# A two-layer streaming encoder on one core: the differential layer's attention scored in head pairs, on a new slot plan, with one row-maximum instruction a pair and a new order of the output projection

## The chip, the cores and the metric

One core of a Trainium2 chip runs the whole program. The metric is the device time of one execution in microseconds, the median of several runs. The profiled execution is one more run, and the rows below come from it.

## What is computed

One inference step of two layers over 576 frames (512 of a prompt, 64 new frames of a running stream with 256 cached ones), width 1024. Layer 0 uses differential attention, layer 1 forgetting attention; each is followed by a SwiGLU FFN.

```python
# layer 0 (of each chunk-causal group of queries)
qkv = h @ w_qkv
q, k = _rope(...), _rope(...)
s = einsum('bqhd,bkhd->bhqk', q, k) * (DIFF_QK_DIM ** -0.5)      # 16 half heads of 64
p = softmax(where(allowed, s, -inf)).reshape(b, DIFF_HEADS, 2, tq, tk)
a = p[:, :, 0] - lam * p[:, :, 1]
o = einsum('bhqk,bkhe->bqhe', a, v)                               # 8 heads, 128 wide
o = rmsnorm(o, subln_w) * (1.0 - lam_init)
x = x + o.reshape(b, t, DIFF_V_WIDTH) @ w_o
x = x + (silu(gate) * up) @ w_out      # gate, up = split(rmsnorm(x) @ w_in)
```

## The kernel before

All matmul operands are split in a high part (fp32r) and a low rest, and a product is hi x hi + lo x hi + hi x lo. Activations lie as columns: 8 tiles of 128 features x 576 frames. Weights come in units of 8 blocks of 128 x 128 through two buffers. For each unit SP loads `w_raw`, ACT makes `w_hi` (`split`, called by `lead`, L787), POOL makes `w_lo` (`lead`, L1069), and PE uses it (`slice_`, L486): per block six matmuls of 288 columns. A slot is one such block. A buffer is free again when PE has used its unit, so hi and lo of unit n + 1 are made while PE is in unit n.

Both attention layers go over 8 groups g of 128 features: three units (k, q, v) in 24 slots, and into the slots of group g the attention of group g - 1 is put, by hand. `S_AT` gives the slots of the ten score jobs: five query blocks i in the order 4, 3, 2, 1, 0 with 384, 512, 384, 256 and 128 keys, for each of the two half heads. `T_AT` gives the slots of the transposes of p, and so on. The engines hold the same order each in its own program and meet by semaphores only. Each engine works strictly in the order of its program, so an instruction that waits holds up all that stand behind it.

One score job of layer 0 (`score`, L534 to L542): three matmuls with 64 rows (partitions 0 to 63 or 64 to 127) into bank jj % 2 of `sps`, then the mask with 128 rows. DVE takes the row maximum (`row_max`, L1233), ACT the exponential with its sum (`exps`, L866). After the second half head DVE weighs and subtracts the two (`weigh`: reciprocal of both, L1248, L1252). PE transposes the result (L554), ACT and DVE take the high part (`take_p`, L882) and the rest (`p_lo`, L1269). There are four buffers `pr`. The head's output is normed: `o_square` on POOL, `head_norm_sum` on PE (L604), `head_scale` on ACT, `norm_o` and `split_o` on DVE, `o_hi` on ACT. k and q of the next group pass `take_k`, `swap`, `rotate`, `k_hi`, `k_lo` and the same for q.

The output projection of a layer is 64 blocks, in the order of `WO_STEPS` (run, output tile, k), in 8 units. A run accumulates in one of two banks, and its end is added to x by DVE (`residual`, L1173); a run opens when the run before the last has been added. Blocks of head 7 (k = 7) come last. The norm for the FFN needs, tile by tile, `prep`: on ACT `xh` (L805), then, once `acc` holds the tile before, the square into the single buffer `sqt` (L809); on DVE `xl` (L1159) and `acc` += `sqt` (L1164). `norm_sum` (L505) adds `acc` over the partitions, `scale_of_norm` makes the factor `rs`. In ACT's program of before, the order at the end is prep of tile 0, lead(u + 6), preps 1 to 4, lead(u + 7), preps 5 to 7, lead(u + 8); lead(u + 7) is the first FFN unit.

## Time and profile before

| | us |
|---|---|
| median of 3 runs | 1607.16 (1603.75 to 1608.9) |
| the profiled execution | 1607.57 |
| its span, first to last instruction | 1605.4 |
| PE busy | 1563.1 (97%) |
| DVE, ACT, POOL busy | 619.9, 560.9, 581.5 |
| granted TensorE clock, mean | 0.991 |

The shares of the span say which engine is full on average. Where it isn't, the stretches and the timeline say what it waits for. In a timeline row "x2" joins two instructions that follow each other; two 288-column matmuls shown as 0.42 us overlap in the pipeline, and the distance from one row's start to the next is what they cost PE.

### The profile page before, as it was taken

How to read it: one execution, taken by the hardware profiler on the slowest of the kernel's cores; microseconds unless marked ns; L12 is line 12 of the kernel's file. 1: busy time of each engine (PE TensorE's matmuls, PEld its weight loads, DVE VectorE, ACT ScalarE, POOL GpSimd, SP SyncE). 2: the span in 40 equal slices, each digit the busy share in tenths (PEclk: the TensorE clock that was granted, in tenths of full speed). 3: DMA queues.
4: the chain of work that ended last, by engine and by line, in shares of the span. 5: the costliest groups of instructions: out<-in, count | busy, mean ns of one | idle time of the engine just before them, and what ended most of it. 6: DMA issues, size and time to landing. Idle time of an engine off the chain costs nothing.

```text
span 1605.4 us, 29879 instructions
## 1 busy us (share of the span) xinstructions
PE 1563.1 (97%) x11071; PEld 1476.8 (92%) x11071; DVE 619.9 (39%) x1091; ACT 560.9 (35%) x995; POOL 581.5 (36%) x276
## 2 busy tenths in 40 slices
PE   6999999999999999999999999999999999999996
PEld 5888888999999999999978888888999999999996
DVE  6667776451111111121366666665521111111212
ACT  4455545442222222222334444444332222232221
POOL 3333233334544444333322222221344455444331
PEclk9999999999999999999999999999999999999998
DMA  5322223122222222222211211111122222222222
GB/s 188 98 85 83 95 85 107 41 79 79 78 82 88 78 78 85 76 82 85 94 62 61 62 60 60 60 57 48 67 79 85 85 78 78 91 78 74 83 83 82
DMA packets 44628, 128.49 MB, mean 80 GB/s; under 512 B 5648, under 2 KB 10256, under 8 KB 44576
## 3 DMA queue, kind: packets, MB, share of 16 engines
q1 hardware_dynamic: 44576, 127.79, 23.6%
q8 instruction: 34, 0.56, 0.1%
q14 instruction: 18, 0.15, 0.0%
HBM read 111.21 MB, written 11.83 MB: 77 GB/s over the span
## 4 chain that ended last, share of the span: by engine, by line
PE 91%; DVE 5%; issue 2%; ACT 1%; DMA 1%; SPq 0%; DVEq 0%; ACTq 0%
PE ps L486 73%; PE sps L534 3%; PE ops L597 3%; PE tps L554 2%; PE sps L540 2%; PE sps L535 2%; PE sps L536 2%; PE sps L542 1%; PE ops L587 1%; DVE acc L1164 1%; DVE aug_l L1303 1%; DVE xT L1173 0%; PE tps L568 0%; DVE ptl L1269 0%; PE ops L604 0%
## 5 line engine op out<-in xcount | busy, mean ns | idle before, releaser
L1069 POOL TENSOR_TENSOR w_lo<-w_raw,w_hi 128x1024 fp32r<-128x1024 f32 (+1 forms) x199 | 469.4, 2359 | 922.2 <-ACT w_hi L787 922.2
L486 PE MATMUL ps<-xh,w_hi 128*128 128x288 f32 x2176 | 489.5, 307 | 18.5 <-DVE xl L1418 11.5
L486 PE MATMUL ps<-xl,w_hi 128*128 128x288 f32 x2176 | 468.7, 297 | 0.0
L486 PE MATMUL ps<-xh,w_lo 128*128 128x288 f32 x2176 | 468.3, 297 | 0.0
L486 PEld LDWEIGHTS ps<-xh,w_hi 128*128 128x128 f32 x2176 | 350.2, 191 | 20.4 <-issue 19.9
L787 ACT ACTIVATE w_hi<-w_raw 128x1024 fp32r<-128x1024 f32 (+1 forms) x200 | 208.3, 1042 | 451.7 <-PE ps L486 449.5
L486 PEld LDWEIGHTS ps<-xh,w_lo 128*128 128x128 f32 x2176 | 352.9, 190 | 0.0
L486 PEld LDWEIGHTS ps<-xl,w_hi 128*128 128x128 f32 x2176 | 352.8, 190 | 0.0
L866 ACT ACTIVATE pr<-sps,nmax 128x384 f32<-128x384 f32 (+3 forms) x160 | 85.9, 537 | 205.4 <-DVE nmax L1233 188.4
L486 PE MATMUL ps<-hh,w_hi 128*128 128x288 f32 x704 | 150.9, 295 | 0.0
L486 PE MATMUL ps<-hl,w_hi 128*128 128x288 f32 x704 | 150.8, 295 | 0.0
L486 PE MATMUL ps<-hh,w_lo 128*128 128x288 f32 x704 | 150.7, 295 | 0.0
L1179 DVE TENSOR_TENSOR uf<-ps,rs 128x576 f32<-128x576 f32 x44 | 33.4, 758 | 238.7 <-PE ps L486 238.7
L1487 DVE TENSOR_TENSOR hl<-hf,hh 128x576 f32 (+1 forms) x44 | 33.4, 758 | 228.7 <-ACT hh L1036 228.7
L1173 DVE TENSOR_TENSOR xT<-ps,xT 128x576 f32<-128x576 f32 (+1 forms) x40 | 30.2, 756 | 232.0 <-PE ps L486 231.7
L486 PEld LDWEIGHTS ps<-hl,w_hi 128*128 128x128 f32 x704 | 113.8, 188 | 0.0
L486 PEld LDWEIGHTS ps<-hh,w_hi 128*128 128x128 f32 x704 | 113.7, 188 | 0.0
L486 PEld LDWEIGHTS ps<-hh,w_lo 128*128 128x128 f32 x704 | 113.5, 188 | 0.0
L1233 DVE TENSOR_REDUCE nmax<-sps 128x1 f32<-128x384 f32 (+3 forms) x160 | 79.5, 500 | 88.0 <-PE sps L542 87.6
L1036 ACT ACTIVATE hh<-hf 128x576 f32 (+1 forms) x44 | 30.2, 686 | 178.3 <-POOL hf L1126 178.3
L534 PE MATMUL sps<-kh,qh 64*128 64x384 f32 (+3 forms) x160 | 66.8, 418 | 2.7 <-ACT qh L837 1.3
L1126 POOL TENSOR_TENSOR hf<-sg,uf 128x576 f32<-128x576 f32 x44 | 62.7, 1426 | 0.0
(154 smaller groups left out, 1768.6 us busy)
## 6 DMA issues: line engine op xcount, KB each, us to landing
w_raw<-w_units SPq DMA_DIRECT2D x184, 512.0 KB, 3.2
w_raw<-w_units SPq DMA_DIRECT2D x16, 384.0 KB, 2.8
qsw<-qsin SPq DMA_DIRECT2D x64, 72.0 KB, 2.0
xT<-x_in SPq DMA_DIRECT2D x8, 288.0 KB, 5.6
dk_out<-kf SPq DMA_DIRECT2D x8, 288.0 KB, 2.1
dv_out<-vf SPq DMA_DIRECT2D x8, 288.0 KB, 4.1
fk_out<-kf SPq DMA_DIRECT2D x8, 288.0 KB, 4.1
fv_out<-vf SPq DMA_DIRECT2D x8, 288.0 KB, 4.0
```

The costliest lines, as they stand in the source:

```text
L486: mm = nc.tensor.matmul(out[:, half, :], w[:, k, :], rhs[:, kt, half * HALF:(half + 1) * HALF], start=start and w is w_hi[slot] and rhs is ...
L534: nc.tensor.matmul(out, qh[par][b, q], kh[par][b, k], start=True, stop=False)
L535: nc.tensor.matmul(out, qh[par][b, q], kl[par][b, k], start=False, stop=False)
L536: nc.tensor.matmul(out, ql[par][b, q], kh[par][b, k], start=False, stop=False)
L597: mm = nc.tensor.matmul(ops[:, P * j:SEQ], v[:, j, :], p[:, j, P * j:SEQ], start=j == 0 and v is vh and p is pth, stop=j == 3 and v is vl)
L787: nc.scalar.activation(w_hi[slot][:, 0:kts, :], w_raw[slot][:, 0:kts, :], ACT.Copy).then_inc(w_hi_done, 1)
L866: nc.scalar.activation(pr[:, slot, 0:width(i)], sps[:, jj % 2, 0:width(i)], ACT.Exp, bias=nmax[:, slot:slot + 1], accum_out=den[:, slot:sl ...
L1069: nc.gpsimd.tensor_tensor(w_lo[slot][:, 0:kts, :], w_raw[slot][:, 0:kts, :], w_hi[slot][:, 0:kts, :].bitcast(F32), ALU.subtract).then_inc( ...
L1126: nc.gpsimd.tensor_tensor(hf[:], sg[:], uf[:], ALU.mult).then_inc(hf_done, 1)
L1179: tt(halves(dst), proj(n.c % 2), halves(scale), ALU.mult).then_inc(ps_read, 1)
L1233: nc.vector.tensor_reduce(nmax[:, slot:slot + 1], sps[:, jj % 2, 0:width(i)], AX_X, ALU.max, negate=True).then_inc(max_done, 1)
L1487: tt(at(hl, jt), hf[:], at(hh, jt).bitcast(F32), ALU.subtract).then_inc(hl_done, 1)
```

## The change

The first layer's attention gets its own program on every engine, written out for all 8 groups, on a time line t of slots; the second keeps its loops. In layer 0:

- `score_pair` scores both half heads in one slot, matmul by matmul in turn, then both masks. It starts when the exps of the pair before are done. Slots 2, 6, 10, 14, 18.
- `pair_max` takes both heads' row maxima with one reduction over both banks.
- the weighing takes the two reciprocals apart: `weigh_first` needs the first exp only.
- transposes of v stand at slot 6, of p at 8, 12, 16, 20, 24; the p x v product of the prompt at slot 27, the head's norm at 34 to 38, all counted from the start of the attention's own period; the small norm matmul goes to `tps[:, 3]`.
- `lead` on ACT and POOL stands at the second slot of each unit.

In both layers:

- `WO_STEPS` has 14 runs instead of 12, in another order. Counted from 0, runs 6 to 13 (tiles 0 to 7) end at steps 46, 47, 48, 49, 51, 53, 55 and 63.
- `prep` is spread among the steps (`wo_prep`, `wo_residuals`, `wo_finish`).
- `norm_sum` of the FFN stands in its second unit at k = 2 instead of its first at k = 6; that of layer 1 behind the first unit instead of at k = 6.

```diff
-WO_STEPS = ([(j, 2 + j, k) for j in (0, 1) for k in range(6)] + [(0, 2, 6), (1, 3, 6)]
-            + [(j, 2 + j, k) for j in (2, 3) for k in range(7)]
-            + [(4 + t, t, k) for t in (0, 1) for k in range(7)] + [(4 + t, t, 7) for t in range(6)]
-            + [(4 + t, t, k) for t in (6, 7) for k in range(KT)])
-WO_OPEN = [next(q for q, s in enumerate(WO_STEPS) if s[0] == j) for j in range(12)]
-WO_END = [max(q for q, s in enumerate(WO_STEPS) if s[0] == j) for j in range(12)]
-WO_EARLY = 9
+N_WO, N_IN, N_OUT, N_LAYER = 24, 38, 82, 90
+WO_STEPS = ([(j, 4 + j, k) for j in (0, 1, 2) for k in range(6)]
+            + [(j, j - 2, k) for j in (3, 4, 5) for k in range(7)]
+            + [(6, 0, k) for k in range(KT)]
+            + [(6 + t, t, 7) for t in (1, 2, 3)]
+            + [(6 + t, t, k) for t in (4, 5, 6) for k in (6, 7)]
+            + [(13, 7, k) for k in range(KT)])
+WO_RUNS = 14
+WO_OPEN = [next(q for q, s in enumerate(WO_STEPS) if s[0] == j) for j in range(WO_RUNS)]
+WO_END = [max(q for q, s in enumerate(WO_STEPS) if s[0] == j) for j in range(WO_RUNS)]
+WO_WITHIN = [j for j in range(WO_RUNS) if WO_END[j] % KT != KT - 1]
...
-S_AT = {DIFF: [0, 1, 3, 4, 7, 8, 11, 12, 15, 16], FOX: [0, 1, 3, 5, 8, 10, 12, 14, 16, 18]}
-T_AT = {DIFF: [6, 9, 13, 17, 21], FOX: [4, 6, 8, 10, 12, 14, 17, 19, 21, 23]}
+D_SCORE, D_WEIGH, D_TURN = (2, 6, 10, 14, 18), (5, 9, 13, 17, 21), (8, 12, 16, 20, 24)
+D_VT, D_PVS, D_PVP, D_HEAD_SUM, D_HEAD_NORM, D_SPLIT_O = 6, 13, 27, 34, 36, 38
+D_K, D_ROT_K, D_K_LO, D_Q, D_ROT_Q, D_Q_LO, D_V = 8, 12, 14, 16, 20, 22, 24
...
-                    if k == 6 and norm > 0:
-                        norm_sum(norm)
...
+            def score_pair(a, par, p):
+                i = JOBS[DIFF][2 * p][0]
+                if some(a * 10 + 2 * p):
+                    pe.wait_ge(exp_done, val(a * 10 + 2 * p))
+                if p == 0:
+                    for s in (qh_done, ql_done, kh_done, kl_done):
+                        pe.wait_ge(s, val(a + 1))
+                q = slice(P * i, P * i + P)
+                k = slice(SEQ, TK) if i == 4 else slice(0, width(i))
+                for x, y, first in ((qh, kh, True), (qh, kl, False), (ql, kh, False)):
+                    for h in range(2):
+                        b = slice(64 * h, 64 * h + 64)
+                        nc.tensor.matmul(sps[:, h, 0:width(i)], x[par][b, q], y[par][b, k], start=first, stop=False)
+                d = 0 if i == 4 else i
+                for h in range(2):
+                    nc.tensor.matmul(sps[:, h, P * d:P * d + P], ident16, mask[DIFF], start=False, stop=True
+                                     ).then_inc(s_done, 1)
...
+            def diff_attention(t):
+                for a in range(G):
+                    s, par, n = t - SLOTS * (a + 1), a % 2, Num(a)
+                    if s == D_PVP:
+                        pv_prompt(DIFF, n, 0)
+                    if s == D_HEAD_SUM:
+                        if a < G - 1:
+                            pe.wait_ge(vr_done, (a + 2) * 2)
+                        pe.wait_ge(pt_lo, t_index(DIFF, min(a + 1, G - 1), 0 if a < G - 1 else 4) + 1)
+                        head_norm_sum(n)
+                    if s == D_VT:
+                        transpose_v(DIFF, n)
+                    for p in range(5):
+                        if s == D_SCORE[p]:
+                            score_pair(n, par, p)
+                    for tt in range(5):
+                        if s == D_TURN[tt]:
+                            if tt == 0:
+                                pe.wait_ge(vr_done, (a + 1) * 2)
+                            if tt == 1 and a > 0:
+                                pe.wait_ge(oln_done, a)
+                            transpose_p(DIFF, n, par, tt)
+                    if s == D_PVS:
+                        pv_sample(DIFF, n, 0)
...
+                    norm_sum(2)
...
+                    if k == NORM_AT:
+                        norm_sum(2 * L + 1)
...
+            def diff_attention(t):
+                for a in range(G):
+                    s, par, n = t - SLOTS * (a + 1), a % 2, Num(a)
+                    if s == D_PVP:
+                        take_o(DIFF, n, 0)
+                    if s == D_HEAD_SUM:
+                        head_scale(n)
+                    if s == D_HEAD_NORM + 1:
+                        o_hi(n)
+                    if s == D_VT + 1:
+                        take_v(DIFF, n)
+                    for tt in range(5):
+                        if s == D_TURN[tt]:
+                            take_p(DIFF, n, tt)
+                    for p in range(5):
+                        if s == D_SCORE[p] + 1:
+                            exps(DIFF, n, par, 2 * p)
+                            exps(DIFF, n, par, 2 * p + 1)
+                    if s == D_PVS:
+                        take_o_sample(DIFF, n, 0)
+            def diff_layer():
+                scale_of_norm(0)
+                for t in range(SLOTS * G + len(WO_STEPS)):
+                    g, s = t // SLOTS, t % SLOTS
+                    if t % KT == 1 and t >= KT:
+                        lead(Num(t // KT))
+                    diff_attention(t)
+                    if g < G:
+                        if s == D_ROT_K + 1:
+                            k_hi(DIFF, Num(g), g % 2)
+                        if s == D_ROT_Q + 1:
+                            q_hi(DIFF, Num(g), g % 2)
+                    else:
+                        wo_prep(DIFF, t - SLOTS * G)
+            def wo_prep(L, q):
+                for k in range(KT):
+                    if WO_END[6 + k] + 1 == q or (k == KT - 1 and q == len(WO_STEPS) - 1):
+                        act.wait_ge(ps_read, N_LAYER * L + N_WO + 6 + k + 1)
+                        prep(2 * L + 1, Num(k))
...
-                lead(u + 3)
-                lead(u + 5)
-                for k in range(KT):
-                    act.wait_ge(ps_read, N_LAYER * L + N_WO + 4 + k + 1)
-                    prep(2 * L + 1, Num(k))
-                    if k == 0:
-                        lead(u + 6)
-                    if k == 4:
-                        lead(u + 7)
...
+                    for q in range(SLOTS + 2 * KT, len(WO_STEPS)):
+                        if q % KT == 1 and q > 6 * KT:
+                            lead(u + q // KT)
+                        wo_prep(L, q)
...
+            def diff_layer():
+                for t in range(SLOTS * G + len(WO_STEPS)):
+                    if t % KT == 1 and t >= KT:
+                        lead(Num(t // KT))
+                    for a in range(G):
+                        s, n = t - SLOTS * (a + 1), Num(a)
+                        if s == D_PVP + 1:
+                            o_square(n)
+                        if s == D_VT + 2:
+                            v_lo(DIFF, n)
...
+            def pair_max(a, par, p):
+                sa = (10 * par + 2 * p) % 4
+                dve.wait_ge(s_done, a.c * 10 + 2 * p + 2)
+                nc.vector.tensor_reduce(nmax[:, sa:sa + 2], sps[:, :, 0:width(JOBS[DIFF][2 * p][0])], AX_X, ALU.max,
+                                        negate=True).then_inc(max_done, 2)
+            def weigh_first(a, par, p):
+                w, tau, sa = width(JOBS[DIFF][2 * p][0]), a.c * 5 + p, (10 * par + 2 * p) % 4
+                dve.wait_ge(exp_done, a.c * 10 + 2 * p + 1)
+                nc.vector.reciprocal(rden[:, sa:sa + 1], den[:, sa:sa + 1]).then_inc(rden_done, 1)
+                dve.wait_ge(rden_done, 2 * tau + 1)
+                nc.vector.tensor_scalar(pr[:, sa, 0:w], pr[:, sa, 0:w], rden[:, sa:sa + 1], None, ALU.mult
+                                        ).then_inc(pa_done, 1)
+            def weigh_second(a, par, p):
+                w, tau, sa = width(JOBS[DIFF][2 * p][0]), a.c * 5 + p, (10 * par + 2 * p) % 4
+                s_b = sa + 1
+                dve.wait_ge(exp_done, a.c * 10 + 2 * p + 2)
+                nc.vector.reciprocal(rden[:, s_b:s_b + 1], den[:, s_b:s_b + 1]).then_inc(rden_done, 1)
+                dve.wait_ge(rden_done, 2 * tau + 2)
+                tt(nlr[:, s_b:s_b + 1], rden[:, s_b:s_b + 1], nlam[:, 5:6], ALU.mult).then_inc(nlr_done, 1)
+                dve.wait_ge(nlr_done, tau + 1)
+                dve.wait_ge(pa_done, tau + 1)
+                stt(pr[:, sa, 0:w], pr[:, s_b, 0:w], nlr[:, s_b:s_b + 1], pr[:, sa, 0:w], ALU.mult, ALU.add
+                    ).then_inc(p_ready, 1)
...
+            def diff_attention(t):
+                for a in range(G):
+                    s, par, n = t - SLOTS * (a + 1), a % 2, Num(a)
+                    if s == D_HEAD_NORM:
+                        norm_o(n)
+                    if s == D_SPLIT_O:
+                        split_o(n)
+                    for p in range(5):
+                        if s == D_SCORE[p] + 1:
+                            pair_max(n, par, p)
+                        if s == D_WEIGH[p]:
+                            weigh_first(n, par, p)
+                            weigh_second(n, par, p)
+                    for tt_ in range(5):
+                        if s == D_TURN[tt_]:
+                            p_lo(DIFF, n, tt_)
+                    if s == D_PVS + 1:
+                        o_sum(DIFF, n, 0)
+            def diff_layer():
+                for t in range(SLOTS * G + len(WO_STEPS)):
+                    for g in range(G):
+                        s, par, n = t - SLOTS * g, g % 2, Num(g)
+                        if s == D_K:
+                            take_k(DIFF, n)
+                        if s == D_ROT_K:
+                            rotate(n, 0)
+                        if s == D_Q:
+                            take_q(DIFF, n)
+                        if s == D_ROT_Q:
+                            rotate(n, 1)
+                        if s == D_V:
+                            take_v(DIFF, n)
+                    if t >= SLOTS * G:
+                        wo_residuals(DIFF, t - SLOTS * G)
+                    diff_attention(t)
+                    for g in range(G):
+                        s, par, n = t - SLOTS * g, g % 2, Num(g)
+                        if s == D_K_LO:
+                            k_lo(DIFF, n, par)
+                        if s == D_Q_LO:
+                            q_lo(DIFF, n, par)
+            def wo_residuals(L, q):
+                for j in range(WO_RUNS - 1):
+                    if WO_END[j] + 1 == q:
+                        if WO_END[j] % KT == KT - 1:
+                            dve.wait_ge(w_used, U_LAYER * L + U_WO + (WO_END[j] + 1) // KT)
+                        else:
+                            dve.wait_ge(wo_done, len(WO_WITHIN) * L + WO_WITHIN.index(j) + 1)
+                        residual(Num(N_LAYER * L + N_WO + j), Num(WO_STEPS[WO_END[j]][1]))
+                if q == WO_END[6]:
+                    clear_acc(2 * L + 1)
+                for k in range(5):
+                    if q == (52, 57, 59, 61, 63)[k]:
+                        prep(2 * L + 1, Num(k))
+            def wo_finish(L):
+                dve.wait_ge(w_used, U_LAYER * L + U_IN)
+                residual(Num(N_LAYER * L + N_WO + WO_RUNS - 1), Num(WO_STEPS[-1][1]))
+                for k in range(5, KT):
+                    prep(2 * L + 1, Num(k))
```

## Rows read from the trace of the kernel before

**Rows 1.** The page: busy us, share of the span, instructions.

```profile
PE 1563.1 (97%) x11071; PEld 1476.8 (92%) x11071; DVE 619.9 (39%) x1091; ACT 560.9 (35%) x995; POOL 581.5 (36%) x276
```

**Rows 2.** Stretches: us, busy (instructions) of PE, PEld, DVE, ACT, POOL, clock, DMA.

```profile
167.50:201.00 33.50, 33.50 (x226) 29.20 (x225) 24.23 (x48) 17.04 (x40) 10.39 (x5) 1.00 0.29 90
...
301.50:345.50 44.00, 41.38 (x299) 39.88 (x298) 24.40 (x29) 17.69 (x26) 15.84 (x7) 1.00 0.19 67
```

**Rows 3.** Timeline of PE, a 512-wide score: start, duration, line, operation, idle before.

```profile
245.72 0.51 PE L486 MATMUL ps<-xh,w_hi 128*128 128x288 f32 x2
...
246.69 0.50 PE L534 MATMUL sps<-kh,qh 64*128 64x512 f32 x1
247.03 0.39 PE L535 MATMUL sps<-kl,qh 64*128 64x512 f32 x1
247.26 0.39 PE L536 MATMUL sps<-kh,ql 64*128 64x512 f32 x1
247.59 0.23 PE L542 MATMUL sps<-csth 128*128 128x128 bf16 x1
247.63 0.51 PE L486 MATMUL ps<-xh,w_hi 128*128 128x288 f32 x2
```

**Rows 4.** Timeline of PE, a 128-wide score.

```profile
265.14 0.52 PE L486 MATMUL ps<-xh,w_hi 128*128 128x288 f32 x2
...
266.29 0.27 PE L535 MATMUL sps<-kl,qh 64*128 64x128 f32 x1
266.40 0.27 PE L536 MATMUL sps<-kh,ql 64*128 64x128 f32 x1
...
266.64 0.51 PE L486 MATMUL ps<-xh,w_hi 128*128 128x288 f32 x2
```

**Rows 5.** Groups by form, DVE, 67 to 301 us: busy us, mean ns | idle.

```profile
L1221 DVE TENSOR_TENSOR kl<-kf,kh 128x896 fp32r<-128x896 f32 x7 | 21.5, 3066 | 0.0
L1252 DVE SCALAR_TENSOR_TENSOR pr<-pr,nlr 128x384 f32<-128x384 f32 x14 | 20.3, 1452 | 1.5
L1233 DVE TENSOR_REDUCE nmax<-sps 128x1 f32<-128x384 f32 x28 | 15.5, 553 | 12.0 <-PE sps L542 12.0
L1233 DVE TENSOR_REDUCE nmax<-sps 128x1 f32<-128x512 f32 x14 | 9.7, 691 | 19.4 <-PE sps L542 19.4
```

**Rows 6.** Groups by form, ACT, the same stretch.

```profile
L787 ACT ACTIVATE w_hi<-w_raw 128x1024 fp32r<-128x1024 f32 x21 | 22.0, 1049 | 0.0
L866 ACT ACTIVATE pr<-sps,nmax 128x384 f32<-128x384 f32 x28 | 16.3, 581 | 19.3 <-DVE nmax L1233 19.2
```

**Rows 7.** Timeline, DVE beside POOL in a period of the first layer.

```profile
225.17 2.38 POOL L1069 TENSOR_TENSOR w_lo<-w_raw,w_hi 128x1024 fp32r<-128x1024 f32 x1 [8.61 <-ACT w_hi L787]
...
225.39 2.57 DVE L1252 SCALAR_TENSOR_TENSOR pr<-pr,nlr 128x384 f32<-128x384 f32 x1
```

**Rows 8.** Timeline, the first output projection's end and the FFN's first matmul.

```profile
331.72 2.95 DVE L1164 TENSOR_TENSOR acc<-acc,sqt 128x576 f32<-128x576 f32 x1
...
334.70 0.69 ACT L809 ACTIVATE sqt<-xT 128x576 f32<-128x576 f32 x1 [2.79 <-DVE acc L1164]
...
339.83 1.04 ACT L787 ACTIVATE w_hi<-w_raw 128x1024 fp32r<-128x1024 f32 x1
...
340.95 2.40 POOL L1069 TENSOR_TENSOR w_lo<-w_raw,w_hi 128x1024 fp32r<-128x1024 f32 x1 [6.90 <-ACT w_hi L787]
...
344.55 0.74 DVE L1173 TENSOR_TENSOR xT<-ps,xT 128x576 f32<-128x576 f32 x1
...
345.51 0.50 PE L486 MATMUL ps<-xh,w_hi 128*128 128x288 f32 x2 [2.19 <-issue]
```

**Rows 9.** Stretch behind that wait; the granted clock is the third number from the end.

```profile
346.30:349.30 3.00, 3.00 (x15) 3.00 (x15) 2.09 (x4) 1.28 (x3) 0.00 (x0) 0.51 0.00 0
```

**Rows 10.** Timeline, norm and forget projection at the second layer's start.

```profile
775.68 1.21 PE L505 MATMUL sps<-acc,cstf 128*128 128x288 f32 x4 [0.27 <-DVE acc L1164]
...
777.70 0.69 ACT L817 ACTIVATE rs<-rs 128x576 f32<-128x576 f32 x1
...
778.53 0.51 PE L660 MATMUL sps<-xh,f_hi 128*128 128x288 f32 x2
```

More of the change, by code:

```diff
@@ L619, in attention @@
[L619 to L620 removed]
+                    if S_AT[FOX][jj] == slot:
+                        score(a, par, jj)
+                for tt in range(len(T_AT[FOX])):
+                    if T_AT[FOX][tt] == slot:
                         if tt == 0:
[L622 to L625 removed]
@@ L955, in group @@
                         scale_of_norm(2)
-                    if alone and L == DIFF and slot == 0:
-                        scale_of_norm(0)
-                    if alone and L == FOX and slot == 13:
+                    if alone and slot == 13:
                         forget()
@@ L1304, in aug_left @@
                                             ).then_inc(aug_l_done, 1)
-            def attention(L, a, par, slot, first=False):
-                if slot == 0 and L == FOX and not first:
-                    o_lo(a - 1, 1)
-                if L == DIFF and not first:
-                    if slot == SS_AT + 2:
-                        norm_o(a - 1)
-                    if slot == SS_AT + 4:
-                        split_o(a - 1)
+            def diff_attention(t):
[16 more added lines that the diff above has]
+                        o_sum(DIFF, n, 0)
@@ L1327, in attention, with group @@
+                for t in range(len(T_AT[FOX])):
+                    if T_AT[FOX][t] == slot:
+                        p_lo(FOX, a, t)
+                for h in range(2):
+                    if PVS_AT[FOX][h] == slot:
+                        o_sum(FOX, a, h)
+                    if PVS_AT[FOX][h] + 2 == slot:
                         o_lo_sample(a, h)
-                    if PVP_AT[L][h] == slot:
+                    if PVP_AT[FOX][h] == slot:
                         o_lo(a, h)
-            def group(L, g, par, first=False, alone=False):
+            def group(g, par, first=False, alone=False):
@@ L1332, in group @@
                 for slot in range(SLOTS):
                     if not alone:
-                        attention(L, g - 1, 1 - par, slot, first)
+                        fox_attention(g - 1, 1 - par, slot, first)
                     if slot == 8:
-                        take_k(L, g)
-                    if slot == 9 and alone and L == FOX:
+                        take_k(FOX, g)
+                    if slot == 9 and alone:
                         forget_1()
-                    if slot == ROTATE_AT[0] and L == DIFF:
-                        rotate(g, 0)
@@ L1353, in group @@
-                take_v(L, g)
+                    if slot == K_LO_AT[FOX]:
+                        k_lo(FOX, g, par)
+                    if slot == (2 * KT if alone else TAKE_Q_AT[FOX]):
+                        take_q(FOX, g)
+                    if slot == 17 and alone:
+                        forget_2()
+                    if slot == Q_AT[FOX]:
+                        q_lo(FOX, g, par)
+                        aug_left(g)
+                take_v(FOX, g)
             def forget_1():
```

465 lines of the change are left out of this document (210 added, 255 removed).

## Prediction, made before the changed kernel was run

> **What bounds the kernel now.** I read the busy shares first: PE 1563.1 us of 1605.4, twice any other engine [rows 1]. The stretches show where it isn't full: a head pair's period in the first layer (33.5 us, PE busy throughout) is issue-bound, and the end of each output projection with the start of the FFN idles 2.6 of 44 us [rows 2]. So time can go only by fewer PE microseconds, or by less idling. Full PE says nothing of how near the others are, though: DVE is at 24.23 us of a 33.5 us period.
>
> **Score blocks.** A slot with nothing but projection takes 0.80 us (six matmuls, two every 0.267 us). The 512-wide score block stretches one to 247.63 - 245.72 = 1.91, so costs 1.11; its three matmuls stream 0.23 each (247.03 to 247.26), 0.69 together, and about 0.42 goes to entering and leaving the 64-row form and to the mask [rows 3]. The 128-wide block costs 266.64 - 265.14 - 0.80 = 0.70, with matmuls 0.11 apart, where the weight load sets the pace [rows 4]. With 0.93 and 0.75 for 384 and 256 columns (the same differences in the same view), a period's ten blocks take 2 x (1.11 + 2 x 0.93 + 0.75 + 0.70) = 8.84 us. `score_pair` enters and leaves once per pair. If the two heads' matmuls still run one after the other, a pair saves about 0.4, 1.9 a period. If they run at the same time, the streaming halves too: 4.84 is left, 3.8 to 4.0 saved. If only the weight loads queue, 2.9. No row of before shows two adjacent matmuls in different 64 rows, so both ends stay open; I take the upper, since the two write different banks and read different partitions.
> The Trainium skill (TensorEngine Tiling, "Key Properties") says that different tiles run LdWeights and Matmul in parallel and that a change of tiling mode drains TensorE. The 0.1 us gaps around the block agree with the second; the first is unshown here. By it alone the layer would give back 8 x 3.8 = 30 us.
>
> **Who is late next.** The pair's two banks come free only when both exps are done, and from slot 8 to slot 20 the work is one serial chain. Zero is PE's entry into slot 8. DVE's maxima of pair 1 are one reduction of 1024 elements: 0.69 for 512 and 0.55 for 384 give 0.14 per 128, so 1.25 (two took 1.38), and ACT's two exps end at 1.3 [rows 5, 6]. ACT's order is then `take_p` (to 1.5), `lead` at slot 9 (1.05), and POOL's w_lo holds from 2.6 to 5.0. DVE's order is `take_k`, `p_lo`, two reciprocals with their waits, `stt` on pr at 2.8. An stt that starts 0.2 us into a w_lo took 2.57 instead of about 0.6, ending 0.4 behind it [rows 7]. So pair 1 is weighed at 5.5; max 2 6.4; exps 2 7.7; `take_p`, `p_lo` 8.9; weigh 2 10.4; `split_o`, `o_sum`, `k_lo` (about 1.05 without a w_lo) 12.2; max 3 12.9; exps 3 14.0. PE, at nominal slots, wants score 4 at 12.7: it waits 1.3. Again `take_p`, `lead`, w_lo from 15.4 to 17.8, and the 256-wide stt ends at 18.1, where PE wants `turn` 3 at 16.5: 1.7. Period: 33.5 - 3.8 + 3.1 = 32.8 if the heads overlap; without overlap PE comes later by 0.9 and 0.3 at these points, 31.6 + 1.9 = 33.5. So the layer is bounded by this chain, and most of the score gain is lost. The chain's small steps (0.15 to 0.8 us) are from the same two views.
> The Trainium skill (SBUF, "Who interferes with whom") calls the port pair of DVE and GpSimd an exclusive lock for a whole instruction; rows 7 agree.
> Sum over eight attentions: the first lacks `norm_o` and `split_o` (saves 2.3), six save 0.7 (4.2), the last runs without `take_k`, `take_q`, `rotate` and `k_lo` (1.7): 8.2. The later start of the first attention shortens its wait for qh by some 0.7.
>
> **The end of each output projection, in both layers.** The new step list and ACT's order go together badly. Let zero be step 47.
> (a) ACT's order is prep(0), prep(1) at step 48, `lead` of the unit that PE needs at step 56, prep(2). prep(1)'s square waits for acc of tile 0, and DVE puts prep(0) at step 52, behind the residual of the run ending there. PE passes 52 at 4.5 (two waits of 0.25 for one-step runs inside; before, such waits cost 0.9 together: 0.28, 0.27 and 0.36 in the same view). Then residual 0.15 + 0.75, xl 0.8, acc 0.75, sqt 0.69, w_hi 1.04, w_lo 0.15 + 2.40: 11.2 to 11.7, with DVE's xl 1 in POOL's way. PE wants it at 7.7. Wait: 3.5 to 4.0. Before, w_hi of that unit stood ahead of prep(1), and acc and sqt blocked each other without harm [rows 8].
> (b) prep(6) at step 56 stands ahead of `lead` at 57, which is the first FFN unit. Its square waits for acc of tile 5, and that stands in `wo_finish`, behind the residual of the last run, so behind the end of the projection. From that end: residual 0.9, xl 0.8, acc 0.7, sqt 0.7, w_hi 1.05, w_lo 2.5 = 6.65 us in which PE has nothing. Before, PE waited 2.19 there, for the residual at 344.55 [rows 8].
> (c) After the 2.19 us wait the granted clock was 0.51 for 3 us, the lower level of 1.2 GHz, and two matmuls took 0.48 instead of 0.267, about 1.5 us in all [rows 9]. Two longer waits now: 3.3 instead of 1.5, with 1.5 to 2.7 for the longer one.
> (d) norm_sum at the second unit brings `scale_of_norm` 3.2 us later and the third unit's split behind it: 0.3 to 0.4.
> Per layer: new 0.5 + 3.9 + 6.65 + 3.3 + 0.35 = 14.7; old 0.9 + 2.2 + 1.5 = 4.6; net 10.1, so 20.2, or 17 to 23. Two more residuals a layer (0.75 each) hide under PE.
>
> **Second layer's start.** norm_sum moves behind the first unit, and the forget projection waits for Ln and Exp, 1.43 us and two gaps, which two slots of projection covered. Without its 0.27 us wait, the norm matmuls (1.0) and a 0.2 gap PE would be through eight slots at 776.9; the norm matmuls end at 777.8 and r_ready comes 1.75 later, so 779.6 against 778.53 [rows 10]: +1.1. The rest of that layer's attention isn't touched. The unrolled code of layer one is at nothing: the straight parts of before show no gap.
>
> **Sum.** 1605.4 - 8.2 - 0.7 + 20.2 + 1.1 = 1617.8 us of span. The profiled execution took 1607.57, 2.2 above its span, and 0.4 above the median of the runs (1607.16). So about 1620.
>
> **Rivals.**
> - No overlap of the heads (0.15): the chain hides most of it, the layer saves 1 to 2 instead of 8: 1627, up to 1630.
> - The short waits of 1.3 and 1.7 us inside each period lower the granted clock as the 2.19 us one did (0.15). Six periods x 1.5 us more: 1629. Against it, 33.5 us periods never dropped; for it, two waits of 1.3 each near 38 and 40 us stood just before a slow stretch.
> - The chain does not bind (0.15): if the stt gets the port before w_lo in both places, weigh 1 is done at 3.5, and each period keeps its 3.8: 1605.4 - 0.7 - 30.4 + 20.2 + 1.1 + 2.2 = 1597.8. The gap between stt (2.8) and w_lo (2.6) is 0.2 us, so this is the one on the other side; it decides at DVE's arrival before POOL's.
> - One of the two collisions only, or a smaller wait at (a) (0.13): about 1608, no difference.
> The forecast has 0.42. From about 0.3% (5 us) on, a measurement of this kernel can tell a change from none. Faster: 0.13, the third rival without its upper tail. Same: 0.17, the fourth and the edges of the first and third. Slower: 0.70. Forecast alone: 1613 to 1627. Eight in ten, with the first two rivals and half of the faster one: 1600 to 1631.
>
> **What would show it.** Right: PE idle 6 to 7 us at each FFN start, released by w_lo, and 3.5 to 4 us eight steps earlier; granted clock near 0.5 behind both; in the first layer 64-row matmuls of the two heads starting together, a period near 32.8, PE's waits at score 4 (for ACT's pr) and `turn` 3 (for DVE's pr), with stt rows of 2.5 us. Wrong: a period near 29.7 without waits (the chain), L535 to L536 spacing of 0.23 for each head in turn (the overlap), or w_hi of the first FFN unit ahead of the last residual (the order).

## The result and the profile after

The changed kernel takes 1633.3 us (median of 4 runs, 1632.6 to 1637.1), before took 1608.0 beside it: a ratio of 1.0166, 95% interval 1.0139 to 1.0192. The forecast was 1620 with a range of 1600 to 1631, so the sign was right, the loss half of what came, and the time stands 2 us outside the range. The profiled run took 1633.27 us with a span of 1631.5, 26.1 more than before's 1605.4.

The page's busy line of the kernel after, for [rows 1]:

```profile
PE 1546.0 (95%) x11071; PEld 1469.6 (90%) x11071; DVE 636.1 (39%) x1095; ACT 554.3 (34%) x995; POOL 582.0 (36%) x276
```

PE is busy 17 us less than before and the span is 26 longer: it idles 43 us more. So the first question is not what the new layout costs PE, but whom PE waits for.

In what follows pairs are counted from 0, score 4 is the score of the last pair, and `turn` 3 is PE's transpose of the weighed pair 3 (L596). Stretches of after: two head periods of the first layer, from `turn` 3 to `turn` 3, then 2.9 us at the beginning of the second of them, then 3 us behind each of the two waits at the end of the first projection. Columns as in [rows 2]; the granted clock is the third number from the end.

```profile
208.96:242.10 33.14, 29.96 (x225) 26.93 (x225) 25.03 (x48) 16.18 (x39) 10.40 (x5) 1.00 0.29 92
242.10:276.99 34.89, 31.40 (x224) 28.43 (x225) 25.03 (x48) 16.18 (x39) 10.66 (x5) 0.95 0.28 87
242.70:245.60 2.90, 2.90 (x14) 2.90 (x14) 2.39 (x8) 1.37 (x6) 0.00 (x0) 0.50 0.45 167
346.30:349.30 3.00, 3.00 (x13) 3.00 (x14) 2.98 (x5) 1.74 (x3) 0.00 (x0) 0.50 0.49 173
361.85:364.85 3.00, 3.00 (x12) 3.00 (x13) 3.00 (x2) 0.00 (x0) 2.75 (x1) 0.50 0.51 175
```

A period was 33.5 us with PE busy throughout [rows 2]. Now PE needs 29.96 and idles 3.2. And there are two kinds of period: one of 33.1 us at full clock, and one of 34.9 in which the first 2.9 us run at 0.50, the lower level of 1.2 GHz (a slow stretch, below). Four of the six periods between the turns at 71.05 and 276.99 us begin so; together they are 205.9 us, against 201 before.

PE's two waits and what they wait for inside such a period (timeline; the bracket tells the idle time before and what ended it):

```profile
204.66 0.33 PE L559 MATMUL sps<-kh,qh 64*128 64x128 f32 x2 [1.16 <-ACT pr L932]
...
206.01 2.36 POOL L1167 TENSOR_TENSOR w_lo<-w_raw,w_hi 128x1024 fp32r<-128x1024 f32 x1 [10.67 <-ACT w_hi L853]
206.14 2.24 DVE L1365 TENSOR_TENSOR nlr<-rden,nlam 128x1 f32<-128x1 f32 x1
208.42 0.48 DVE L1368 SCALAR_TENSOR_TENSOR pr<-pr,nlr 128x256 f32<-128x256 f32 x1
...
208.96 0.44 PE L596 MATMUL tps<-cstf,pr 128*128 128x128 f32 x2 [1.90 <-DVE pr L1368]
```

These are the two waits of the forecast, at score 4 (forecast 1.3, here 1.16) and at `turn` 3 (1.7, here 1.90). The row to remember is the third: a product of one column, which takes 0.16 us elsewhere, took 2.24 beside POOL's `w_lo`, which had begun 0.13 us earlier. The forecast had put the collision one instruction later, on the `stt` (SCALAR_TENSOR_TENSOR, L1368), and left this product out of DVE's list. The `stt` took 0.48. Of the 16 weighings of pairs 1 and 3 the product was held in 15, for 2.14 to 2.32 us, the `stt` in none. All that DVE does behind it, and PE's turn, come 2 us later.

The score block (512 keys), for [rows 3]:

```profile
255.48 0.50 PE L559 MATMUL sps<-kh,qh 64*128 64x512 f32 x2
255.82 0.40 PE L559 MATMUL sps<-kl,qh 64*128 64x512 f32 x2
256.05 0.40 PE L559 MATMUL sps<-kh,ql 64*128 64x512 f32 x2
256.38 0.28 PE L562 MATMUL sps<-csth 128*128 128x128 bf16 x2
```

"x2" are the two heads; both start at the row's time, and the next pairs follow 0.34 and 0.23 us later, as one head's matmuls did before. The heads overlap.

The end of the first projection, for [rows 8]: first the unit of step 56, then the first FFN unit.

```profile
341.25 0.75 DVE L1271 TENSOR_TENSOR acc<-acc,sqt 128x576 f32<-128x576 f32 x1
...
342.04 0.69 ACT L875 ACTIVATE sqt<-xT 128x576 f32<-128x576 f32 x1 [4.34 <-DVE acc L1271]
342.63 1.04 ACT L853 ACTIVATE w_hi<-w_raw 128x1024 fp32r<-128x1024 f32 x1
...
343.74 2.34 POOL L1167 TENSOR_TENSOR w_lo<-w_raw,w_hi 128x1024 fp32r<-128x1024 f32 x1 [10.95 <-ACT w_hi L853]
...
346.19 0.58 PE L512 MATMUL ps<-oh,w_hi 128*128 128x288 f32 x1 [3.38 <-POOL w_lo L1167]
...
355.37 0.76 DVE L1280 TENSOR_TENSOR xT<-ps,xT 128x576 f32<-128x576 f32 x1 [3.47 <-PE ps L512]
...
356.90 0.75 DVE L1271 TENSOR_TENSOR acc<-acc,sqt 128x576 f32<-128x576 f32 x1
...
357.69 0.68 ACT L875 ACTIVATE sqt<-xT 128x576 f32<-128x576 f32 x1 [4.39 <-DVE acc L1271]
358.28 1.04 ACT L853 ACTIVATE w_hi<-w_raw 128x1024 fp32r<-128x1024 f32 x1
...
359.39 5.21 POOL L1167 TENSOR_TENSOR w_lo<-w_raw,w_hi 128x1024 fp32r<-128x1024 f32 x2 [13.31 <-ACT w_hi L853]
...
361.85 0.58 PE L512 MATMUL ps<-xh,w_hi 128*128 128x288 f32 x1 [6.52 <-ACT w_hi L853]
```

Both chains are the forecast's (a) and (b), step by step, with waits of 3.38 and 6.52 us, and both are followed by a stretch at half clock. The profile names ACT's `w_hi` at the second wait, but that had ended at 359.32; the first of the two `w_lo` in the row above it ended at 361.75, 0.10 us before PE went on.

Where the 26 us stand, by PE's events that both kernels have (before, after, difference added since the line above):

| event | before | after | added |
|---|---|---|---|
| third unit's opening | 38.19 | 39.81 | +1.6 |
| first score | 40.53 | 44.43 | +2.3 |
| first FFN unit | 345.51 | 361.85 | +12.4 |
| forget projection (layer 2) | 778.53 | 796.54 | +1.7 |
| first FFN unit of layer 2 | 1165.21 | 1191.85 | +8.6 |
| final norm | 1592.88 | 1620.01 | +0.5 |

One microsecond comes back behind the final norm.

### The profile page after: what moved, and what is told of

It reads as the page before. It is cut to its first block, busy times and chain, and to the rows that moved or that the text cites. A ratio compares the mean times of both kernels' runs of the same rounds, so it can differ in the third digit from the quotient of the medians.

```text
span 1631.5 us, 29340 instructions
## 1 busy us (share of the span) xinstructions
PE 1546.0 (95%) x11071; PEld 1469.6 (90%) x11071; DVE 636.1 (39%) x1095; ACT 554.3 (34%) x995; POOL 582.0 (36%) x276
## 4 chain that ended last, share of the span: by engine, by line
PE 74%; DVE 3%; issue 2%; ACT 1%; POOL 1%; DVEq 0%; ACTq 0%; POOLq 0%
PE ps L512 63%; PE ops L638 2%; PE sps L582 2%; PE sps L577 2%; PE tps L596 1%; PE sps L579 1%; PE sps L578 1%; PE ops L628 1%; POOL w_lo L1167 1%; DVE aug_l L1424 0%; PE sps L725 0%; DVE ptl L1388 0%; ACT w_hi L853 0%; PE sps L584 0%; DVE ql L1332 0%
## 5 line engine op out<-in xcount | busy, mean ns | idle before, releaser
L596 PE MATMUL tps<-cstf,pr 128*128 128x128 f32 x312 | 55.1, 277 | 19.3 <-DVE pr L1368 16.5
L512 PE MATMUL ps<-oh,w_hi 128*128 128x288 f32 x256 | 59.7, 315 | 7.4 <-POOL w_lo L1167 6.8
L1388 DVE TENSOR_TENSOR ptl<-tps,pth 128x512 fp32r<-128x512 f32 (+1 forms) x96 | 47.0, 489 | 46.9 <-ACT pth L948 45.9
```

What stands on the lines that cost most here:

```text
L512: mm = nc.tensor.matmul(out[:, half, :], w[:, k, :], rhs[:, kt, half * HALF:(half + 1) * HALF], start=start and w is w_hi[slot] and rhs is ...
L596: mm = nc.tensor.transpose(tps[:, b, :], pr[:, slot, P * b:P * b + P], ident)
L1388: tt(dst, src, hi.bitcast(F32), ALU.subtract).then_inc(pt_lo, 1)
```

## Experiments

All kernels below start from the changed kernel. The runs of the kernel before that stood beside them had medians of 1607.1 to 1608.9 us. Where two kernels are compared that ran beside different ones of these, 1 or 2 us of the difference of their medians can come from that, and the text says so.

**ACT's order at the projections' ends.** In both layers the `lead` of the unit used at step 56 goes from step 49 to 48, and that of the first FFN unit from 57 to 56, ahead of the preps there:

```diff
-                    if t % KT == 1 and t >= KT:
+                    if t % KT == 1 and KT <= t < SLOTS * G + 6 * KT:
...
+                if q in (6 * KT, 7 * KT):
+                    lead(Num(U_LAYER * L + U_WO + q // KT))
                 for k in range(KT):
-                    if WO_END[6 + k] + 1 == q or (k == KT - 1 and q == len(WO_STEPS) - 1):
+                    if q == (47, 48, 49, 56, 56, 56, 57, 63)[k]:
...
-                        if q % KT == 1 and q > 6 * KT:
-                            lead(u + q // KT)
```

> Changed kernel; only ACT's order at the end of both output projections is mended: the lead of step 49 goes to 48, ahead of the prep of tile 1, the lead of step 57 to 56, ahead of the preps of tiles 3 to 7. My theory (in each layer PE's waits of 3.4 us at step 56 and 6.5 us at the first FFN unit come from a weight split that stands behind a square which waits for acc): both waits vanish, and the slow stretches behind them (11 and 7 rows of 0.48 instead of 0.267 us, some 3.8 us) with them. In return the split of the second FFN unit now stands behind the last square, which waits for acc of tile 6 (4.0 us behind the end), so PE waits about 2 us there and loses 1.5 us to the clock. Net 9 to 10 us a layer: 1613 to 1616 us. Rival 1, the residual's own end or POOL is what PE waits for: the waits stay, 1633. Rival 2, the clock falls there whatever PE waits for: only the 10 us of waits less 2 go, 8 a layer with the slow stretches staying: 1620.

Measured: 1619.2 us, ratio 1.0074 (1.0054 to 1.0095), 14.1 us less than the changed kernel. In its trace the forget projection comes 9.8 us earlier and the final norm 17.0. The two waits are gone, and the third one came where it was expected (second FFN unit, timeline of this kernel):

```profile
356.35 1.05 ACT L853 ACTIVATE w_hi<-w_raw 128x1024 fp32r<-128x1024 f32 x1
...
357.47 2.34 POOL L1167 TENSOR_TENSOR w_lo<-w_raw,w_hi 128x1024 fp32r<-128x1024 f32 x1 [8.25 <-ACT w_hi L853]
359.91 0.37 PE L512 MATMUL ps<-xh,w_hi 128*128 128x288 f32 x1 [2.28 <-issue]
```

So the order is the cause of the two waits, and rival 1 falls. In this trace the first layer's two slow stretches went with them; in the second layer one of 3.3 us at 0.50 stands behind the new wait. The time missed its forecast of 1613 to 1616: the median stands at rival 2's 1620. The profiled run was the fastest of the four (1616.3, mean granted clock 0.987 against 0.984 and 0.985 in the others), so the trace speaks against rival 2 in this run, and how many slow stretches the other three had isn't shown.

**DVE's preps earlier.** In addition to the order just mended, and with ACT's prep of tile 3 at step 50 instead of 56, in `wo_residuals` and `wo_finish`:

```diff
-                    if q == (47, 48, 49, 56, 56, 56, 57, 63)[k]:
+                    if q == (47, 48, 49, 50, 56, 56, 57, 63)[k]:
...
-                for k in range(5):
-                    if q == (52, 57, 59, 61, 63)[k]:
+                for k in range(7):
+                    if q == (51, 53, 55, 57, 58, 59, 60)[k]:
...
-                for k in range(5, KT):
+                for k in range(7, KT):
```

> As the first kernel, and DVE's preps of tiles 0 to 6 stand at steps 51, 53, 55, 57, 58, 59, 60 instead of 52, 57, 59, 61, 63 and two behind the end, so that only the last tile's stands behind the last residual. My theory: both waits, the new one at the second FFN unit and the slow stretches all go; each projection end costs less than before's 4.6 us: 11 to 13 us a layer, 1607 to 1611 us. Rival: more DVE work between the residuals delays them, and the runs that open at steps 50 to 56 wait (up to 3 us a layer): 1613 to 1617.

Measured: 1621.2 us, ratio 1.0073 (1.0050 to 1.0097): nothing gained over 1619.2. The wait at the second FFN unit was still 1.96 us, now because the last tile's square and the split behind it wait for the residual itself, and PE waited 1.25 and 0.42 us for residuals at 345.38 and 347.66 us, as the rival had it. In this profile six of the eight waits at `turn` 3 were followed by a slow stretch instead of four, and it was the slowest of the four runs (1623.4). The expectation was wrong by 10 us or more, and the rival's 1613 to 1617 was passed too.

**POOL stands back for the weighing.** In the changed kernel, the first layer's `w_lo` at slots 9 and 17 waits until pairs 1 and 3 are weighed:

```diff
+                    for a in range(G):
+                        for at_, p in ((9, 1), (17, 3)):
+                            if t - SLOTS * (a + 1) == at_:
+                                pool.wait_ge(p_ready, a * 5 + p + 1)
                     if t % KT == 1 and t >= KT:
                         lead(Num(t // KT))
```

> Changed kernel; in the first layer POOL's w_lo at slots 9 and 17 waits in addition until DVE has weighed pair 1 and pair 3. My theory (DVE's small product and its stt lose the port to w_lo twice in a period, 2.2 us each, and this serial chain is what PE waits for, 1.2 us at score 4 and 1.9 us at the turn of pair 3; the granted clock then falls in every second period): DVE's 2.25 us rows of the small product are gone, PE's two waits too, the slow stretches of 1.8 us too, and the period is 30 to 31 us instead of 34.0 on average (33.1 and 35.0 by turns): 7 periods less 3 to 4 us, 1605 to 1612. Rival 1, w_lo moved 0.7 us later blocks the next DVE instructions of the chain (k_lo, the rotation of q) as long: waits move, 1625 to 1633. Rival 2, the clock falls whatever the waits are: 1615 to 1618 with slow stretches left in four periods.

Measured: 1609.7 us, ratio 1.0014 (1.0004 to 1.0024), 23.6 us less from two waits a period on an engine that was itself not late, inside the expected 1605 to 1612. Its timeline, and the stretch of that period:

```profile
160.23 0.16 DVE L1369 TENSOR_TENSOR nlr<-rden,nlam 128x1 f32<-128x1 f32 x1
160.42 0.48 DVE L1372 SCALAR_TENSOR_TENSOR pr<-pr,nlr 128x256 f32<-128x256 f32 x1
...
160.99 2.39 POOL L1167 TENSOR_TENSOR w_lo<-w_raw,w_hi 128x1024 fp32r<-128x1024 f32 x1 [9.35 <-DVE pr L1372]
...
162.23 1.76 DVE L1328 TENSOR_TENSOR qf<-qf,qsw 128x576 f32<-128x576 f32 x1 [0.99 <-DMA qsw<-qsin]
...
165.42 0.33 PE L596 MATMUL tps<-cstf,pr 128*128 128x128 f32 x1 [0.84 <-DVE pr L1372]
```

```profile
165.42:196.86 31.44, 29.91 (x224) 26.88 (x225) 22.54 (x48) 16.40 (x39) 10.45 (x5) 1.00 0.32 96
```

The small product is back at 0.16 us, the turn of pair 3 waits for nothing, score 4 waits 0.24 us instead of 1.2, no period has a slow stretch. What `w_lo` blocks now is the rotation of q (1.76 instead of 0.75 us), and PE waits 0.84 us one turn later. That is the part of rival 1 which is true. The period, 31.4 us, is longer than the 30 to 31 expected.

**The same at slot 17 only**, so that the wait of 1.2 us at score 4 stays and that of 1.9 goes (the list in the diff above is `((17, 3),)`).

> Changed kernel, POOL's additional wait at slot 17 alone (for the weighing of pair 3); slot 9 as in the changed kernel. Which of the two waits brings the clock down? Theory A, the longer one at the turn (1.9 us): it shrinks to 0.8 or less, the wait of 1.2 us at score 4 stays, no slow stretch in any period from 70 us on: the period is 32.2 to 32.5 throughout, 1633.3 less 7 x 1.6 = 1622 (1619 to 1624). Theory B, any wait of 1 us or more does, score 4's too: slow stretches stay in about every second period, now behind score 4, 1627 to 1630.

Measured: 1618.9 us, ratio 1.0074 (1.0054 to 1.0093), at the lower edge of theory A's 1619 to 1624. The wait at score 4 is there in the six inner periods, 1.14 to 1.20 us (0.32 in the first and 0.15 in the last), and none of them has a slow stretch; one of them:

```profile
202.94:235.33 32.39, 30.00 (x224) 26.89 (x225) 22.86 (x48) 16.27 (x39) 10.41 (x5) 1.00 0.31 99
```

Theory A: the slow stretches go with the longer wait. Over the four profiles that have it (the changed kernel and those with the mended order, the earlier preps and the two maxima), waits of 1.9 us at a turn were followed by half clock in 19 of 30 cases; waits of 0.8 to 1.2 us at turns and scores in none. What apart from the length decides over the other eleven isn't shown.

**Two maxima a pair**, which undoes the change that the title names:

```diff
-                nc.vector.tensor_reduce(nmax[:, sa:sa + 2], sps[:, :, 0:width(...)], AX_X, ALU.max,
-                                        negate=True).then_inc(max_done, 2)
+                for h in range(2):
+                    dve.wait_ge(s_done, a.c * 10 + 2 * p + h + 1)
+                    nc.vector.tensor_reduce(nmax[:, sa + h:sa + h + 1], sps[:, h, 0:width(...)],
+                                            AX_X, ALU.max, negate=True).then_inc(max_done, 1)
```

> Changed kernel with the pair's one reduction over both banks taken apart again into one for each head; nothing else. The one reduction took 1.22 us for 2 x 512, 0.95 for 2 x 384, 0.69 for 2 x 256 elements; two should take 0.69, 0.55 and 0.42 each. Theory A (the reduction is on PE's chain, and it holds the first exponential back until both heads are reduced): the first exp starts 0.3 to 0.5 us earlier in each pair, PE's two waits in a period shrink from 3.1 together to some 1 to 2, and two or more of the four slow stretches go: 1618 to 1628. Rival B (w_lo's collision moves with the chain and hides it): within 2 us of 1633. Rival C (the second instruction's fixed part is what counts, 0.15 us a pair on a full chain): 1635 to 1638.

Measured: 1625.5 us, ratio 1.0104 (1.0083 to 1.0126), 7.8 us less than with one instruction. The wait at score 4 fell from 1.2 to 0.44 us or nothing, that of the turn stayed at 1.9 (`w_lo` sets it), the one inner period without slow stretch took 32.3 us instead of 33.1. The time is theory A's (1618 to 1628): the joint reduction holds the first exponential back. Its part on the clock didn't come: five of the six waits of 1.9 us were followed by a slow stretch here, where it wanted two or more of the four gone. That also says that the wait at the turn is enough by itself, since the one at score 4 had all but gone.

**Both mends together**, ACT's order and POOL's two waits.

> The two mends that gained together: ACT's order at the end of both output projections, and POOL's w_lo waits at slots 9 and 17 of the first layer. Apart they gave 14.1 and 23.6 us. If the two causes are separate, as my accounting has it: 1633.3 - 37.7 = 1595.6 (1593 to 1598), a period of 31.3 us, and 8 to 10 us less behind each projection. If part of both gains was one and the same (the clock behind the end of the layer), 1600 or more.

Measured: 1593.9 us, ratio 0.9922 (0.9901 to 0.9943). The sum holds within 2 us: two separate causes, and what is left of the layout without them is a gain.

On top of both mends, three single edits:

> As e6_both, with two maxima a pair again. On the changed kernel this gave 8 us. If that was the chain of waits being 0.3 to 0.5 us shorter a pair and two clock stretches with it, here, where the period waits 1.1 us only and the last wait hangs on the rotation of q, it gives 0 to 3: 1591 to 1594. If the second instruction's head start is worth the same wherever it stands: 1586.

Measured: 1593.0 us, ratio 0.9907 (0.9875 to 0.9938). Here the second maximum gives 0.9 us by the medians, 2.4 by the two ratios (this kernel ran beside a before of 1608.9, the one with both mends beside 1607.1), which is no more than the runs scatter, against 7.8 where the chain set PE's time.

> As e6_both, with DVE's k_lo of group 0 behind take_q. Theory: k_lo waits 1.1 us for kh and takes 1.1, and take_q's sine product, its swap, the rotation and qh stand behind it, so the first score's wait of 2.8 us falls to about 0.7: 1.8 to 2.2 us less than e6_both, 1592. Rival (kl then becomes the late one, or the unit opened behind is late anyway): no change.

The edit is `if s == (D_K_LO if g else D_Q): k_lo(...)`. Measured: 1590.3 us, ratio 0.9893 (0.9862 to 0.9924), 3.6 us less (4.7 by the ratios), more than the 1.8 to 2.2 expected; the first score, first in the changed kernel and then here:

```profile
36.34 1.09 DVE L1328 TENSOR_TENSOR kl<-kf,kh 128x896 fp32r<-128x896 f32 x1 [1.10 <-ACT kh L894]
37.35 0.75 DVE L1291 TENSOR_TENSOR qsin<-ps,sinr 128x576 f32<-128x576 f32 x1
...
44.43 0.55 PE L559 MATMUL sps<-kh,qh 64*128 64x384 f32 x2 [2.81 <-ACT qh L903]
```

```profile
34.07 0.75 DVE L1295 TENSOR_TENSOR qsin<-ps,sinr 128x576 f32<-128x576 f32 x1
...
41.13 0.45 PE L559 MATMUL sps<-kh,qh 64*128 64x384 f32 x2 [0.49 <-issue]
```

The wait fell by 2.3 us. The rest of the difference between these two traces is the slow stretch at 21 us, which this profile did not have. Nor does it have the one that all profiles with the wait of 2.8 us show behind the first score (from 44.62 us in the changed kernel, some 1.5 us by the price that the prediction took from [rows 9]). That would account for the surplus, but wasn't taken apart.

**Do the heads overlap because they alternate?** As with both mends, but head by head:

```diff
-                for x, y, first in ((qh, kh, True), (qh, kl, False), (ql, kh, False)):
-                    for h in range(2):
+                for h in range(2):
+                    for x, y, first in ((qh, kh, True), (qh, kl, False), (ql, kh, False)):
```

> As e6_both, with the six 64-row matmuls of a pair head by head (three of head 0, three of head 1) instead of by turns; the masks as before. What do the turns give, where the chain hides little? If the two heads' matmuls overlap only when they alternate: 1.9 to 2.0 us more PE time a period, of which the wait of 0.84 at the last turn and 0.25 at score 4 take up 1.1, so 0.9 to 2.0 x 8 = 7 to 16 us: 1603 to 1611. If head 1's first matmul runs beside head 0's last either way and the width is covered: within 3 us of e6_both.

Measured: 1594.6 us, ratio 0.9925 (0.9906 to 0.9943), the same as with turns, and the trace shows the same pairs starting together, although head 1's first matmul is now the fourth in the program:

```profile
206.36 0.51 PE L559 MATMUL sps<-kh,qh 64*128 64x512 f32 x2
206.70 0.41 PE L559 MATMUL sps<-kl,qh 64*128 64x512 f32 x2
206.94 0.40 PE L559 MATMUL sps<-kh,ql 64*128 64x512 f32 x2
```

**Is it an overlap at all?** As with both mends, but `b = slice(0, 64)` for both heads. The second head's own scores are left out by this, so the result is another; it is there for its time only:

> As e6_both, but the second head's six-matmul share reads the first 64 rows of q and k, as the first head's does, so the second head's scores are the first head's again (the result is another). Nothing else differs in size, order or banks. In e6_both and in e7_heads_in_turn the two heads' matmuls start together (one row x2, three rows 0.11 to 0.17 us apart). Theory (they overlap because they lie in different 64 rows): here they run one after the other, 0.23 us each for 512 columns, 0.17 for 384, 0.11 for 256 and 128: 3 x (0.23 + 2 x 0.17 + 2 x 0.11) = 2.4 us more PE time a period; the wait of 0.84 at the last turn and 0.25 at score 4 take up 1.1 of it: 1.3 to 2.4 us x 8 = 10 to 19, 1604 to 1613. Rival (the rows' start times only look alike, the engine streams both anyway one after the other): within 3 us of e6_both, 1594.

Measured: 1607.9 us, ratio 0.9999 (0.9986 to 1.0012), 14.0 us more by the medians, 12.4 by the ratios. Its timeline:

```profile
181.48 0.73 PE L559 MATMUL sps<-kh,qh 64*128 64x512 f32 x2
182.04 0.62 PE L559 MATMUL sps<-kl,qh 64*128 64x512 f32 x2
182.51 0.62 PE L559 MATMUL sps<-kh,ql 64*128 64x512 f32 x2
```

The pairs now lie 0.56 and 0.47 us apart instead of 0.34 and 0.23, and a period takes 32.85 us instead of 31.42. PE's wait at the last turn fell from 0.84 to 0.31 us and the one at score 4 went: the overlap is worth about 2.2 us of PE a period, of which the chain behind takes some 0.8, and the 1.4 left are 11 us over eight attentions.

**All of it**: both mends, two maxima, the start, and two smaller ones, the split of the second FFN unit ahead of the last square and `norm_sum(2)` back at k = 6 of the second layer's first unit.

> As e6_both, and four smaller edits: two maxima a pair again; in group 0 DVE's k_lo behind take_q (the sine product of q started 3.9 us later than before, 1.8 of it from a slow stretch, 2.1 from this order); the split of the second FFN unit ahead of the last square (2.3 us wait to 1.5); the second layer's norm_sum back at k = 6 of its first unit. Theory: start -2 us, each projection end -0.8, the second layer's start -1.2, the maxima -0.3 to -0.8 in each of 8 periods (PE's wait of 0.84 at the last turn): e6_both less 7 to 11 us, 1585 to 1589. Rival: the maxima's chain isn't what PE waits for at the last turn (the rotation of q beside w_lo is), they give nothing: e6_both less 4 to 5.

Measured: 1584.3 us (1583.95 to 1585.06), ratio 0.9861 (0.9842 to 0.9879), just below the expected 1585 to 1589 and less than both kernels. The three places, by the traces with both mends alone and with all: first score's wait 2.81 to 0.52 us, second FFN unit 2.27 to 1.46, forget projection 1.64 gone with 0.27 in the norm's place.

## Why the prediction was half right

- **Score blocks and overlap**: right. PE needs 29.96 us a period instead of 33.5, and without overlap about 2.2 us of that would be lost again (forecast 1.9 to 2.1). The rest, 3.5 - 2.2 = 1.3 us by subtraction, is about what entering the 64-row form once a pair instead of twice gave; 1.9 was forecast for it.
- **Who is late next**: right in mechanism and size, not in the instruction. Both waits, their places, their releasers and the collision of DVE's weighing with `w_lo` came as worked out, but the `stt` rows of 2.5 us that were to show it didn't: the product ahead of it, which the forecast had left out, met `w_lo` first. The forecast's period of 32.8 adds 3.1 for two waits that make 3.0; at full clock 33.1 was measured, and the sum over the six periods is 2 us short by that.
- **The rival that the chain does not bind** (1597.8) is what POOL's wait made true: it gave 1609.7, since the period came to 31.4 and not 29.7, with 0.84 us still waited for, and since the start and the clock behind it cost more than any rival had.
- **The projections' ends**: (a) 3.5 to 4.0, measured 3.38; (b) 6.65, measured 6.52; clock (c) half speed behind both. In the second layer, whose attention isn't touched, the table gives 8.6 + 0.5 = 9.1 us for the projection's end and what follows, where 10.1 was forecast. The two layers were put at 20.2; mending the order alone gave 14.1 in the medians and 17.0 in the profiles, while a new wait of 2.28 us a layer kept part of it. The step stands, some 10% too dear.
- **Second layer's start**: +1.1; its wait is 1.64 and the segment +1.7, with the clock behind the FFN's start in it.
- **The step that failed: what is done to the clock in the first layer.** The sum had no term for it. It stood among the rivals at 0.15, with the right place and price (1.5 us a drop, 1629 in all). Four of six periods lost 1.75 us each, 7.0 us. The evidence that I had put against it, that no 33.5 us period ever dropped, said nothing: those periods had no wait. The runs put in its place: 19 of 30 waits of 1.9 us at the turn followed by a slow stretch, and none once POOL's second wait had shortened that one, with the 1.2 us wait still there.
- **The start, the second term that failed**: -0.7 was forecast, measured +3.9 to the first score. Of this 1.6 is a slow stretch at 21 us behind a wait that before had as well; 2.3 is DVE's `k_lo`, which in the new order stands ahead of `take_q` and waits there 1.1 us for `kh`. I had costed this for a full period, where it is hidden, not for the first one.
- The account: forecast 12.4 us of span, measured 26.1. Clock in the periods 7.0, start 4.6, longer periods 2.1 make 13.7, and that is the whole difference. The smaller items (the first and the last attention, the projections' ends a little cheaper) cancel within 2 us; they weren't taken apart, so that the three terms meet the difference to a tenth is luck.
- **The range** ended 2 us short, because the rivals were treated as alternatives to the forecast. The clock's drop was one that adds to the forecast, and forecast plus this rival plus something unseen at the start was the case that came.

## What to carry to other kernels

When a change takes work off a full engine, follow the chain that then becomes due, and look at each small instruction of it for a long one on another engine that can start just ahead: here two waits a period on POOL were worth 24 us. The later `w_lo` made no unit late (the one shown ended at 163.38, 2 us before the turn at 165.42), but it wasn't free: it slowed the rotation of q, and PE waited 0.84 us one turn later. An in-order engine that both prepares the next weights and takes part in a reduction should issue the weights first: here that was worth 14 us. And a wait of about 2 us on TensorE is to be priced with the half-clock stretch that may follow it, as a sum with the other effects and not as a rival to them.

## What the runs showed of the hardware

- Matmuls in different 64 rows run at the same time even when the program puts three of one head before three of the other: both first ones start together (206.36 us above), so a queued matmul of the other half overtakes two that stand ahead of it. The sentence in the description of the kernel before, that each engine works strictly in the order of its program, doesn't hold for PE here. The pairing in the program made no difference (1593.9 and 1594.6 us). The Trainium skill (TensorEngine Tiling (Array Packing), "Key Properties") says that different tiles run independently; these traces agree, and the run with equal rows gives the value, 12 to 14 us.
- A DVE product of a single column is held up by a POOL tensor instruction as long as a wide one: 2.24 us instead of 0.16, for the rest of `w_lo`. The Trainium skill (SBUF — State Buffer, "Who interferes with whom") names as the condition the two inputs in SBUF, not the size; the trace agrees. Reductions from PSUM ran beside `w_lo` undisturbed. In the changed kernel this one began 1.3 us into a `w_lo` and took 0.96 us; the eight that met none took 0.95:

```profile
214.04 2.39 POOL L1167 TENSOR_TENSOR w_lo<-w_raw,w_hi 128x1024 fp32r<-128x1024 f32 x1 [5.67 <-ACT w_hi L853]
...
215.33 0.96 DVE L1346 TENSOR_REDUCE nmax<-sps 128x2 f32<-128x768 f32 x1 [1.65 <-PE sps L562]
```

- The same wait is not always followed by the lower clock: 19 of 30 waits of 1.9 us were, four of eight, at the same turns, in the changed kernel and the one with the mended order, six of eight and five of six in the other two. The 2.3 us wait at the second FFN unit was followed by it in some traces (both mends, at 336.50 us) and not in others (the mended order alone, at 359.91). Single waits of 0.8 to 1.2 us in a period never were, but in the kernel before two of 1.26 and 1.31 us, at 38.19 and 40.53, stood ahead of a drop at 42.6. A forecast can hold only a share here.
